# State-space heads whose two column groups work in pairs, and an FF down projection with the gated activations stationary

## The chip, the cores and the metric

One core of one Trainium2 chip runs the whole program in one launch. The metric is the device time of an execution in microseconds (us), lower is better. Five engines work side by side: PE (matmuls; its weight loads are shown apart as PEld), DVE (vector operations), ACT (activation functions and copies), POOL (hardly used here) and SP (which issues the DMAs).

## The reference, cut to what matters

Two transformer-like blocks run one after the other on 256 tokens of width 1024: first two layers with a mixture of experts, then one layer with three mixers (mLSTM, attention, state space) and a feed-forward net (FF). Only the last two parts are touched.

```python
def ssd_scan(x, dt, a_coef, bm, cm, state, emit):     # 8 heads of width 64, in 2 groups, two directions
    ...
        xdt = xk * dtk[..., None]
        seg = jnp.exp(jnp.where(causal, s[:, :, None] - s[:, None], -jnp.inf))
        y = (jnp.einsum('btsh,bshp->bthp', jnp.einsum('bthn,bshn->btsh', ch, bh) * seg, xdt)
             + jnp.exp(s)[..., None] * jnp.einsum('bthn,bhpn->bthp', ch, h))

def conv_ffn(h, w_up, conv_w, w_down):                # D_FF = 2816
    a, g = jnp.split(dwconv(h @ w_up, conv_w), 2, axis=-1)
    return (jax.nn.silu(g) * a) @ w_down

        h2 = modulate_2(rmsnorm_2(x, norm2_g[l]), mod[3][:, None], mod[4][:, None])
        x = x + mod[5][:, None] * conv_ffn(h2, w_up[l], ffn_conv_w[l], w_down[l])
```

## The kernel before, in words

Activations are held features by tokens (`x` is 128 partitions x 8 x 256). Every engine has its own program, written out by hand in one order; semaphores tie them together. Weights come through a ring of six 1 MB slots that SP refills when a slot is released. Eight PSUM banks serve PE's results: banks 0 to 3 are handed round to ACT (`to_act`), banks 4 to 7 to DVE (`to_dve`); PE may fill a bank again when its reader has taken it (`fill`, `close`, `take`). A float32 matmul shows up as two rows of PE in the trace. An fp32r matmul is one row; there, weights and activations are split into a high and a low part (ACT makes the high one, L1994, DVE the low one, L2896), and `PASSES` multiplies three of the four combinations.

**State-space heads (L1345 to L1368).** For each of 8 heads `hd` and 2 directions `d` a 512 x 256 matrix of decays (4 tiles of 128 x 256) is made: PE spreads a row over the partitions (`s_rows`, L1241), DVE subtracts and caps (`s_least`, L2846), ACT takes the exponential (`s_exps`, L1974), DVE multiplies by the masked products of the head's group (`s_qm`, L2044; made by `mask`, L2630 to L2640). PE then multiplies each tile by the head's values (L1366): 64 output columns, 4 tiles, 2 directions, so 8 float32 matmuls a head, into partitions 0 to 63 for an even head and 64 to 127 for an odd one. DVE takes the result out (`s_out`, L2858). Between two heads PE computes one "spare" slot, a 256-column slice of the merge gates (`linear`, L596: 16 float32 matmuls 256 wide), whose two results ACT takes out with a tanh (L1516). `s_xd` is the values times the time step, 8 DVE operations ahead of head 0. At head 0 and head 4 the products of the next group are made (L1234).

**FF (L1403 to L1454).** After the norm (`norm_sum`, L687; ACT's L1531 and L1535; DVE's L2119; then the split of `h`, ACT L2012 and DVE L2940) PE runs 11 pairs of 128-wide hidden tiles: `up` (L1421) for two weight slots, 96 matmuls 256 wide, and then `down` (L1432) of the pair before, 48 matmuls 256 wide: the weights are stationary and the tokens move, and the results add up over all pairs in banks 4 to 7. Four matmuls of zeros (L1408, 8 rows) open these banks. DVE does the convolution and the gate (L2048, L2053) and writes `f_parts` (L2960, L2044), whose completion is the semaphore `ff_hidden`. After the last `down` DVE adds gate times result to `x` (L2053, 8 operations), PE turns `x` into token order (L1454, 16 transposes), ACT copies that to `o_tok` (L1516) and SP stores it (L1498, 4 DMAs).

## Time and profile before

| | before |
|---|---|
| median of 3 runs | 1795.87 us (1794.08 to 1800.66) |
| the profiled execution: its time | 1794.45 us |
| its span (first to last instruction) | 1792.7 us |
| mean granted TensorE clock | 0.988 of full |
| state-space head blocks (from the first value matmul) | 1434.0 to 1519.7 us of the span |
| FF pairs | 1595.57 to 1786.05 us |
| after the last FF matmul | 1786.05 to 1792.7 us |

All times in the rows below are us from the start of the span; a row of the timeline gives start, duration, engine, line, operation, tiles, shape and count, and in brackets the idle time ahead of it and what ended it. Matmuls are pipelined: the duration of a run of them includes the tail of the last, so their pace is better read from the start of one run to the start of the next.

### The profile page before, as it was taken

The numbers are of one execution on the slowest core, as the hardware profiler recorded it, in microseconds if no ns is written. First come the engines' busy times: TensorE is split into PE (matmuls) and PEld (weight loads), VectorE is DVE, ScalarE is ACT, GpSimd is POOL, SyncE is SP. The second block draws the span as 40 slices with busy tenths as digits, with TensorE's granted clock in tenths as the row PEclk, the third lists the DMA queues.
The fourth block names the chain that finished last, engine by engine and source line by source line (L and its number), as shares of the span: only waits on it lengthen the run. The fifth ranks groups of instructions, "written<-read, shape, count | busy, mean of one in ns | idle before, by whom it ended". The sixth has DMA issues, their size and how long they took to land.

```text
span 1792.7 us, 24286 instructions
## 1 busy us (share of the span) xinstructions
PE 1726.9 (96%) x9797; PEld 1379.6 (77%) x9797; DVE 1158.8 (65%) x1670; ACT 764.7 (43%) x997; POOL 0.2 (0%) x4
## 2 busy tenths in 40 slices
PE   6999899999998999999999989999999999999999
PEld 4798677777886867777778876996745877899998
DVE  3665644448996376644469977528865763679887
ACT  3534533336674344433356756324322442254443
POOL 0000000000000000000000000000000000000000
PEclk9999899999999999999999999999999999999999
DMA  9958667778894696777778971234641332455540
GB/s 353 289 187 297 243 257 280 278 278 312 335 347 166 227 323 230 272 292 278 278 298 323 345 253 51 91 118 141 235 141 50 115 94 94 148 182 188 188 165 25
DMA packets 179032, 393.02 MB, mean 219 GB/s; under 512 B 11365, under 2 KB 102232, under 8 KB 162536
## 3 DMA queue, kind: packets, MB, share of 16 engines
q1 hardware_dynamic: 177246, 390.10, 60.9%
q8 instruction: 78, 1.28, 0.3%
q10 hardware_dynamic: 1674, 1.36, 0.2%
q14 instruction: 34, 0.28, 0.0%
HBM read 390.39 MB, written 1.05 MB: 218 GB/s over the span
## 4 chain that ended last, share of the span: by engine, by line
PE 86%; DVE 6%; ACT 3%; DMA 3%; issue 1%; ACTq 0%; SPq 0%; DVEq 0%
PE bank L969 19%; PE bank L997 10%; PE bank L596 9%; PE bank L1421 7%; PE bank L1208 5%; PE bank L1432 3%; PE bank L981 3%; PE bank L623 3%; PE bank L732 3%; PE bank L640 3%; PE bank L791 2%; PE bank L687 2%; PE bank L656 2%; DMA ring<-in_gla_w_in_dram 2%; PE bank L1012 2%; PE bank L1366 1%
## 5 line engine op out<-in xcount | busy, mean ns | idle before, releaser
L2352 DVE TENSOR_TENSOR parts<-ring,parts 128x2048 fp32r<-128x2048 f32 x144 | 328.7, 2290 | 140.2 <-ACT parts L1722 138.9
L969 PE MATMUL bank<-parts 128*128 128x512 f32 x1536 | 360.4, 393 | 8.4 <-DVE parts L2352 3.3
L1722 ACT ACTIVATE parts<-ring 128x2048 fp32r<-128x2048 f32 x144 | 275.3, 1917 | 204.5 <-PE bank L969 135.6
L969 PEld LDWEIGHTS bank<-parts 128*128 128x128 f32 x1536 | 286.3, 189 | 76.0 <-issue 17.8
L1516 ACT ACTIVATE work<-bank 128x256 f32<-128x256 f32 (+3 forms) x223 | 97.5, 446 | 406.3 <-PE bank L596 66.2
L997 PE MATMUL bank<-parts 128*128 128x512 f32 x768 | 182.9, 396 | 5.7 <-DVE parts L2377 3.7
L997 PEld LDWEIGHTS bank<-parts 128*128 128x128 f32 x768 | 145.5, 191 | 40.4 <-DVE parts L2377 4.1
L596 PE MATMUL bank<-hh,ring 128*128 128x256 f32 x640 | 143.4, 383 | 2.9 <-ACT hh L1563 2.7
L596 PEld LDWEIGHTS bank<-hh,ring 128*128 128x128 f32 x640 | 122.0, 192 | 23.9 <-issue 7.4
L1421 PE MATMUL bank<-parts 128*128 128x256 f32 x1056 | 128.6, 283 | 1.4 <-DVE parts L2940 1.4
L1421 PEld LDWEIGHTS bank<-parts 128*128 128x128 f32 x1056 | 127.6, 192 | 2.2 <-issue 2.2
L2896 DVE TENSOR_TENSOR parts<-ring,parts 128x2048 fp32r<-128x2048 f32 x37 | 84.8, 2292 | 16.7 <-ACT parts L1994 16.2
L1208 PE MATMUL bank<-hh,ring 128*128 128x256 f32 (+1 forms) x256 | 86.6, 491 | 2.2 <-ACT work L1516 2.2
L1994 ACT ACTIVATE parts<-ring 128x2048 fp32r<-128x2048 f32 x37 | 70.7, 1910 | 33.3 <-PE bank L1432 23.8
L2053 DVE SCALAR_TENSOR_TENSOR work<-work,cols 128x256 f32<-128x256 f32 (+1 forms) x144 | 76.2, 529 | 5.1
L2044 DVE TENSOR_TENSOR work<-work 128x256 f32<-128x256 f32 (+10 forms) x122 | 68.8, 564 | 16.0 <-ACT work L1974 6.7
L1208 PEld LDWEIGHTS bank<-hh,ring 128*128 128x128 f32 x256 | 47.4, 190 | 39.6 <-issue 32.9
L2053 DVE SCALAR_TENSOR_TENSOR work<-work 128x256 f32<-128x256 f32 (+4 forms) x96 | 62.6, 653 | 10.1 <-ACT work L1516 3.8
L1432 PE MATMUL bank<-parts 128*128 128x256 f32 x528 | 65.0, 283 | 0.0
L1432 PEld LDWEIGHTS bank<-parts 128*128 128x128 f32 x528 | 64.1, 192 | 0.0
L2126 DVE TENSOR_TENSOR ring_low<-ring,work_rounded 128x1024 fp32r<-128x1024 f32 x36 | 42.5, 1221 | 26.1 <-ACT work_rounded L1594 26.0
L981 PE MATMUL bank<-ring,work 128*64 128x256 f32 x512 | 58.8, 382 | 0.0
(324 smaller groups left out, 2488.8 us busy)
## 6 DMA issues: line engine op xcount, KB each, us to landing
ring<-in_moe_w_gate_dram SPq DMA_DIRECT2D x64, 1024.0 KB, 6.4
ring<-in_moe_w_up_dram SPq DMA_DIRECT2D x64, 1024.0 KB, 7.5
ring<-in_moe_w_down_dram SPq DMA_DIRECT2D x64, 1024.0 KB, 7.0
ring<-in_ada_w_dram SPq DMA_DIRECT2D x48, 1024.0 KB, 7.8
ring<-in_w_in_dram SPq DMA_DIRECT2D x32, 1024.0 KB, 6.0
ring<-in_w_mod_dram SPq DMA_DIRECT2D x24, 1024.0 KB, 7.4
ring<-in_w_up_dram SPq DMA_DIRECT2D x22, 1024.0 KB, 4.9
ring<-in_gla_w_in_dram SPq DMA_DIRECT2D x12, 1024.0 KB, 7.8
```

The lines of the kernel that those rows point to most:

```text
L596: ins = pe.matmul(ps[:, 0:n], w[:, k, m * P:(m + 1) * P], rhs(k), start=k == 0, stop=k == kt - 1)
L969: ins = pe.matmul(bank[:, :], xg[:, a_, k, tile * P:(tile + 1) * P], w[b_][:, j, :], start=k == 0 and n == 0, stop=k == KT - 1 and n == 2)
L981: ins = pe.matmul(bank[64 * h_:64 * h_ + 64, 0:256], x_few[:, k, :], w[:, j, 256 * h_:256 * h_ + 256], start=k == 0, stop=k == KT - 1)
L997: ins = pe.matmul(y_bank(rank, b, n)[:, :], he_t[:, b, a_, q * P:(q + 1) * P], w[b_][:, j, n * 512:(n + 1) * 512], start=i == 0 and q == 0 ...
L1208: ins = pe.matmul(ps[:, 0:n], w[:, k, m * P:(m + 1) * P], rhs(k), start=k == 0, stop=k == KT - 1)
L1421: ins = pe.matmul(ps[:, 0:T], w[a_][:, k, m * P:(m + 1) * P], h_parts[:, b_, k, :], start=k == 0 and i == 0, stop=k == KT - 1 and i == 2)
L1432: ins = pe.matmul(banks[4 + m // 2][:, (m % 2) * T:(m % 2 + 1) * T], w[a_][:, q, m * P:(m + 1) * P], f_parts[:, b_, i % 2, q, :], start=False,
L1516: act.activation(dst, view, func, **kw).then_inc(tiles.taken, 1)
L1722: act.activation(moe_w[:, n % 3, 0, :], ring[:, g % RING, :], ACT.Identity)\
L2053: v(dve.scalar_tensor_tensor(out=o, in0=i0, scalar=sc, in1=i1, op0=op0, op1=op1), done)
L2352: dve.tensor_tensor(moe_w[:, n % 3, 1, :], ring[:, (MOE_AT[layer] + AT[key]) % RING, :], moe_w[:, n % 3, 0, :].bitcast(F32), sub).then_inc ...
L2896: dve.tensor_tensor(w_parts[:, n % 3, 1, :], ring[:, (ff0 + n) % RING, :], w_parts[:, n % 3, 0, :].bitcast(F32), sub).then_inc(sem("low_re ...
```

## The change

1. Heads: the outer loop runs over 9 steps. Step `s` works on direction 1 of head `s-1` and direction 0 of head `s`. The two lie in different halves of the columns, and their matmuls alternate. The fourth tile of either is 128 wide and not 256: the other half of it is masked to zero. So a step has 8 matmuls, 4 in the first and the last. The products of both groups are made ahead of head 0, the second mask lies in the free part of `hh`, and rows and results have fixed banks with semaphores of their own (`s_row`, `s_values`, `s_out`).
2. FF: `down` makes the activations (`f_parts`) stationary and moves the weights 512 wide: 24 matmuls a pair and not 48. The result is in token order, 2 x 2 banks. The first matmul of a bank clears it, so the matmuls of zeros and the memset behind them go.
3. The turn of `x` into token order is done in the pairs 1 to 4 (`tokens_turned`, 4 transposes each, taken by ACT), and the gate is spread over partitions in pairs 5 and 6 (`gate_spread`, 4 float32 matmuls each). At the end DVE multiplies each bank by the gate and adds it to `o_tok` (two operations 512 wide a bank), and SP stores it.

```diff
-            def s_rows(hd):
-                if hd % 4 == 0:
-                    g = hd // 4
-                    products(lambda st: s_x[:, 4 + g, st * P:(st + 1) * P], s_x[:, 6 + g, T:TC])
-                spread(to_dve, (row_r, P, 64 + hd), (row_r, P, 96 + hd))
-                marks["s_row", hd] = to_dve.n
+            def s_products(g):
+                products(lambda st: s_x[:, 4 + g, st * P:(st + 1) * P], s_x[:, 6 + g, T:TC])
...
+            def s_row_bank(step):
+                return banks[4 + (s_first + step % 2) % 4]
+            def s_out_bank(hd):
+                return banks[4 + (s_first + 2 + hd // 2 % 2) % 4]
...
+            def s_rows(step):
+                if step < 2:
+                    pe.wait_ge(to_dve.taken, s_first + step + 1)
+                else:
+                    pe.wait_ge(sem("s_least"), 2 * step - 3)
+                for i, (hd, d) in enumerate(((step - 1, 1), (step, 0))):
+                    if 0 <= hd < S_H:
+                        ins = pe.matmul(s_row_bank(step)[:, i * T:(i + 1) * T],
+                                        ident[:, 64 + 32 * d + hd:65 + 32 * d + hd].to_broadcast([P, P]), row_r[:, :],
+                                        start=True, stop=True)
+                ins.then_inc(sem("s_row"), 1)
+            S_ORDER = ((0, 1, 2, 3), (0, 1, 3, 2))
+            def s_values(step):
+                if step == 0:
+                    pe.wait_ge(sem("s_xd"), 8)
+                    pe.wait_ge(to_dve.taken, s_first + 4)
+                elif 4 <= step < S_H:
+                    pe.wait_ge(sem("s_out"), step - 3)
+                pe.wait_ge(sem("s_w"), min(2 * step + 1, 2 * S_H))
+                for i in range(4):
+                    for hd, d in ((step - 1, 1), (step, 0)):
+                        if 0 <= hd < S_H:
+                            st = S_ORDER[d][i]
+                            at = slice(0, T) if i < 3 else (slice(P, T), slice(0, P))[d]
+                            rows = slice(64 * (hd % 2), 64 * (hd % 2) + 64)
+                            ins = pe.matmul(s_out_bank(hd)[rows, at], s_xd[:, d, st, hd * 64:(hd + 1) * 64],
+                                            s_e[hd % 2][d][:, st, at], start=d == 0 and i == 0, stop=d == 1 and i == 3,
+                                            skip_group_check=True)
+                ins.then_inc(sem("s_values"), 1)
+            s_products(0)
+            s_products(1)
             s_rows(0)
-            for hd in range(S_H):
-                if hd + 1 < S_H:
-                    s_rows(hd + 1)
-                for _ in range(2 if hd == 0 else 1):
+            for step in range(S_H + 1):
+                if step == 0:
                     spare.pop(0)()
-                rows = slice(64 * (hd % 2), 64 * (hd % 2) + 64)
-                ps = to_dve.fill(pe)
-                if hd == 0:
-                    pe.wait_ge(sem("s_xd"), 8)
-                for d in range(2):
-                    pe.wait_ge(sem("s_w"), 2 * hd + d + 1)
-                    for st in range(4):
-                        ins = pe.matmul(ps[rows, 0:T], s_xd[:, d, st, hd * 64:(hd + 1) * 64], s_e[hd % 2][d][:, st, :],
-                                        start=st == 0 and d == 0, stop=st == 3 and d == 1)
-                close(to_dve, ins)
+                if step < S_H:
+                    s_rows(step + 1)
+                    spare.pop(0)()
+                s_values(step)
...
+                    linear("branch", to_dve, lambda k: y[:, k, :], T, kt=4, tiles=4,
+                           after={2: 6, 3: 8} if half == 0 and y is y_m else {})
...
-            pe.wait_ge(sem("f_zeros"), 1)
-            for b in range(4):
-                pe.matmul(banks[4 + b][:, :], f_zero[:, 0:P], f_zero[:, :], start=True, stop=False,
-                          skip_group_check=True)
...
+            def down_part(w, i, q, t, n, order):
+                for a_, b_ in order:
+                    ins = pe.matmul(banks[4 + 2 * t + n][:, :], f_parts[:, b_, i % 2, q, t * P:(t + 1) * P],
+                                    w[a_][:, q, n * 512:(n + 1) * 512], start=i == 0 and q == 0 and (a_, b_) == (0, 0),
+                                    stop=i == FF_PAIRS - 1 and q == 1 and (a_, b_) == (1, 0), skip_group_check=True)
+                return ins
...
-                for q in range(2):
-                    for m in range(KT):
-                        for a_, b_ in PASSES:
-                            ins = pe.matmul(banks[4 + m // 2][:, (m % 2) * T:(m % 2 + 1) * T],
-                                            w[a_][:, q, m * P:(m + 1) * P], f_parts[:, b_, i % 2, q, :], start=False,
-                                            stop=i == FF_PAIRS - 1 and q == 1 and a_ == 1, skip_group_check=True)
-                        if i == FF_PAIRS - 1 and q == 1 and m % 2:
+                if i < FF_PAIRS - 1:
+                    for q in range(2):
+                        for t in range(TT):
+                            for n in range(2):
+                                ins = down_part(w, i, q, t, n, PASSES)
+                    ins.then_inc(sem("ff_down_used"), 1)
+                else:
+                    for t in range(TT):
+                        for n in range(2):
+                            for q in range(2):
+                                ins = down_part(w, i, q, t, n, PASSES)
                             ins.then_inc(sem("ff_done"), 1)
...
+            def gate_spread(half):
+                ps = to_act.fill(pe)
+                for k in range(4):
+                    at = 40 + 4 * half + k
+                    ins = pe.matmul(ps[:, k * P:(k + 1) * P], mods[:, 2, at:at + 1].to_broadcast([P, P]), ident,
+                                    start=True, stop=True)
+                close(to_act, ins)
             for i in range(FF_PAIRS):
                 up("ff_a", first=i == 0)
                 up("ff_g")
                 if i:
                     down(i - 1)
+                if 1 <= i < 5:
+                    tokens_turned((i - 1) // 2, (i - 1) % 2)
+                elif 5 <= i < 7:
+                    gate_spread(i - 5)
             down(FF_PAIRS - 1)
...
-            for half in range(2):
-                for t in range(TT):
+            for t in range(TT):
+                for half in range(2):
                     at = slice(half * 512, (half + 1) * 512)
-                    sp.wait_ge(sem("act_tile_taken"), marks["out", half, t])
+                    sp.wait_ge(sem("x_final"), 2 * t + half + 1)
                     sp.dma_start(out[0, t * P:(t + 1) * P, at], o_tok[:, t, at]).then_inc(sem("stored"), 16)
...
+            def s_exps(step):
+                for hd, d in ((step - 1, 1), (step, 0)):
+                    if 0 <= hd < S_H:
+                        act.wait_ge(sem("s_least"), 2 * hd + d + 1)
+                        r = 64 + 32 * d + hd
+                        for st in range(4):
+                            e = s_e[hd % 2][d][:, st, :]
+                            act.activation(e, e, ACT.Exp, bias=col_c[:, st, r:r + 1]).then_inc(sem("s_exp"), 1)
...
+                if 1 <= i < 5:
+                    take(o_tok[:, (i - 1) // 2, (i - 1) % 2 * 512:(i - 1) % 2 * 512 + 512], n=512)
+                elif 5 <= i < 7:
+                    take(gate_row[:, (i - 5) * 512:(i - 4) * 512], n=512)
...
+            def s_masks(g):
+                for half in range(2):
+                    mask(s_masked[g], half, take())
+            def s_least(step):
+                for i, (hd, d) in enumerate(((step - 1, 1), (step, 0))):
+                    if 0 <= hd < S_H:
+                        r = 32 * d + hd
+                        rows = marks["s_row_bank"](step)[:, i * T:(i + 1) * T]
+                        dve.wait_ge(sem("s_row"), step + 1)
+                        v(dve.tensor_tensor(s_e[hd % 2][d], rows.unsqueeze(1).to_broadcast([P, 4, T]),
+                                            col_n[:, :, r:r + 1].to_broadcast([P, 4, T]), ALU.min), sem("s_least"))
+            def s_weights(step):
+                for hd, d in ((step - 1, 1), (step, 0)):
+                    if 0 <= hd < S_H:
+                        dve.wait_ge(sem("s_exp"), 8 * hd + 4 * d + 4)
+                        tt(s_e[hd % 2][d], s_e[hd % 2][d], s_masked[hd // 4][:, d], mul, done=sem("s_w"))
...
+            for step in range(S_H + 1):
+                s_weights(step)
+                if step > 1:
+                    s_out(step - 2)
+                elif step == 1:
+                    dve.wait_ge(sem("s_values"), 1)
+                if step < S_H:
+                    s_least(step + 1)
...
-            v(dve.memset(f_zero, 0.0), sem("f_zeros"))
...
-            for k in range(KT):
-                if k % 2 == 0:
-                    dve.wait_ge(sem("ff_done"), k // 2 + 1)
-                stt(x[:, k, :], banks[4 + k // 2][:, (k % 2) * T:(k % 2 + 1) * T], mods[:, 2, 40 + k:41 + k],
-                    x[:, k, :], mul, add, done=sem("x_final") if k % 4 == 3 else s["dve_step"])
+            dve.wait_ge(sem("act_tile_taken"), marks["f_rows"])
+            gated = f_c.rearrange("p j t -> p (j t)")[:, 0:512]
+            for t in range(TT):
+                for half in range(2):
+                    at = slice(half * 512, half * 512 + 512)
+                    dve.wait_ge(sem("ff_done"), 2 * t + half + 1)
+                    tt(gated, banks[4 + 2 * t + half], gate_row[:, at], mul)
+                    tt(o_tok[:, t, at], o_tok[:, t, at], gated, add, done=sem("x_final"))
```

`s_exps` and `s_least` go over the same two (head, direction) pairs of a step as `s_weights`; `tokens_turned` holds four transposes of `x` and the hand-over to ACT. The old tail of transposes goes.

How PE's order moves at the first two head blocks. Before, from the products on (L1234 products, L1241 rows, L596 spare slots, L1366 values; the banks are numbered):

```order
L1234 MATMUL bank6<-work 128x256 [waits dve_tile_taken]
L1241 MATMUL bank7<-work,con 128x256 [waits dve_tile_taken]
L1241 MATMUL bank4<-work,con 128x256 [waits dve_tile_taken]
L596 MATMUL bank2<-hh,ring 128x256 [waits act_tile_taken,slot_landed5]
...
L1366 MATMUL bank5<-work 64x256 [waits s_w,s_xd,dve_tile_taken]
L1366 MATMUL bank5<-work 64x256 x3
L1366 MATMUL bank5<-work 64x256 [waits s_w]
L1366 MATMUL bank5<-work 64x256 x3
L1241 MATMUL bank6<-work,con 128x256 [waits dve_tile_taken]
L1241 MATMUL bank6<-work,con 128x256
L596 MATMUL bank2<-hh,ring 128x256 [waits act_tile_taken,slot_landed1]
```

And in the changed kernel (L1237 products, L1371 rows, L599 spare slots, L1392 values), the same place, and a later step in which the two heads have banks of their own:

```order
L1237 MATMUL bank7<-work 128x256 [waits dve_tile_taken]
L1237 MATMUL bank4<-work 128x256 [waits dve_tile_taken]
L1371 MATMUL bank5<-work,con 128x256 [waits dve_tile_taken]
...
L1392 MATMUL bank7<-work 64x256 [waits s_w,dve_tile_taken,s_xd]
L1392 MATMUL bank7<-work 64x256 x2
L1392 MATMUL bank7<-work 64x128
L1371 MATMUL bank5<-work,con 128x256 [waits s_least]
L1371 MATMUL bank5<-work,con 128x256
L599 MATMUL bank2<-hh,ring 128x256 [waits act_tile_taken,slot_landed1]
...
L1392 MATMUL bank7<-work 64x256 [waits s_w]
L1392 MATMUL bank4<-work 64x256
```

The second group's products stand ahead of the first rows, the first value block has 4 matmuls (the last 128 wide) instead of 8, and from then on two heads alternate. The spare slots keep their place ahead of the blocks.

DVE at the same place, changed kernel (L2906 is `s_least`, L2686 to L2696 the masks, L2100 products with the time step, then the weights):

```order
L2906 TENSOR_TENSOR work<-bank,lam_p 128x1024 [waits s_row,dve_tile_taken]
L2686 COPY hh<-bank 128x2x256 [waits dve_tile_ready,s_least]
L2687 COPY hh<-bank 128x2x256 [waits dve_step]
...
L2696 TENSOR_TENSOR hh<-bank,con 128x128 [waits dve_step]
L2100 TENSOR_TENSOR work<-work 128x512 [waits act_tile_taken,dve_tile_taken]
L2100 TENSOR_TENSOR work<-work 128x512 [waits s_xd] x7
L2100 TENSOR_TENSOR work<-work 128x1024 [waits s_exp,s_xd]
L2906 TENSOR_TENSOR work<-bank,lam_p 128x1024 [waits s_row,s_w]
L2906 TENSOR_TENSOR work<-bank,lam_p 128x1024 [waits s_row,s_least]
```

Before, two `s_least` (L2846) stood ahead of the eight products, two weights followed, and the masks of the second group came at head 4:

```order
L2846 TENSOR_TENSOR work<-bank,lam_p 128x1024 [waits dve_tile_ready,dve_tile_taken]
L2846 TENSOR_TENSOR work<-bank,lam_p 128x1024 [waits s_least]
L2044 TENSOR_TENSOR work<-work 128x512 [waits act_tile_taken,dve_tile_taken]
L2044 TENSOR_TENSOR work<-work 128x512 [waits s_xd] x7
L2044 TENSOR_TENSOR work<-work 128x1024 [waits s_exp,s_xd]
L2044 TENSOR_TENSOR work<-work 128x1024 [waits s_exp,s_w]
L2846 TENSOR_TENSOR work<-bank,lam_p 128x1024 [waits dve_tile_ready,s_w]
```

So the masks of the second group now stand ahead of `s_xd`, and one `s_least` and one weight less do.

## Rows read from the trace of the kernel before

**Rows 1.** The page: busy shares of the engines.
```profile
PE 1726.9 (96%) x9797; PEld 1379.6 (77%) x9797; DVE 1158.8 (65%) x1670; ACT 764.7 (43%) x997; POOL 0.2 (0%) x4
```
**Rows 2.** Windows, busy us (x instructions) of PE, PEld, DVE, ACT, POOL, clock, DMA.
```profile
1434.00:1519.70 85.70, 85.50 (x385) 64.85 (x384) 43.27 (x53) 31.24 (x76) 0.00 (x0) 1.00 0.29 94
1595.57:1786.05 190.48, 190.48 (x1584) 190.28 (x1584) 165.46 (x262) 83.41 (x99) 0.00 (x0) 1.00 0.41 139
```
**Rows 3.** Timeline of PE, the first head blocks.
```profile
1418.37 1.89 PE L1241 MATMUL bank<-work,con 128*128 128x256 f32 x8
1420.10 13.98 PE L596 MATMUL bank<-hh,ring 128*128 128x256 f32 x64
1434.01 3.67 PE L1366 MATMUL bank<-work 128*64 128x256 f32 x16
...
1438.94 7.14 PE L596 MATMUL bank<-hh,ring 128*128 128x256 f32 x32 [0.20 <-ACT work L1516]
1446.01 3.67 PE L1366 MATMUL bank<-work 128*64 128x256 f32 x16
1449.61 1.13 PE L1241 MATMUL bank<-work,con 128*128 128x256 f32 x4
```
**Rows 4.** Timeline of PE, expert stage: paired column groups, transposes, 512-wide fp32r.
```profile
249.87 1.09 PE L1022 MATMUL bank<-con,hh 128*128 128x128 f32 x8
250.89 3.67 PE L981 MATMUL bank<-ring,work 128*64 128x256 f32 x32
254.49 11.18 PE L997 MATMUL bank<-parts 128*128 128x512 f32 x48
265.51 0.38 PE L1030 MATMUL bank<-con,work 128*128 128x128 f32 x2
```
**Rows 5.** Timeline of DVE and ACT around the first head block.
```profile
1417.78 0.69 DVE L2630 COPY work<-bank 128x512 f32<-128x512 f32 x1 [0.31 <-PE bank L1234]
1421.70 2.48 DVE L2846 TENSOR_TENSOR work<-bank,lam_p 128x1024 f32<-128x1024 f32 x2
1424.21 8.29 DVE L2044 TENSOR_TENSOR work<-work 128x512 f32<-128x512 f32 x10
1433.80 3.30 ACT L1974 ACTIVATE work<-work 128x256 f32<-128x256 f32 x8 [7.54 <-DVE work L2846]
1437.12 1.28 ACT L1516 ACT_TABLE_LOAD   x1
1438.41 1.21 ACT L1516 ACTIVATE work<-bank 128x256 f32<-128x256 f32 x4
```
**Rows 6.** Timeline of PE and DVE, the last FF pairs.
```profile
1762.85 11.68 PE L1421 MATMUL bank<-parts 128*128 128x256 f32 x96
1774.37 11.68 PE L1432 MATMUL bank<-parts 128*128 128x256 f32 x96
1779.50 0.42 DVE L2044 TENSOR_TENSOR parts<-work,parts 128x256 fp32r<-128x256 f32 x1
```
**Rows 7.** Timeline of all engines after the last FF matmul.
```profile
1788.94 1.23 ACT L1516 ACTIVATE work<-bank 128x512 f32<-128x512 f32 x2 [0.85 <-PE bank L1454]
```
**Rows 8.** Timeline of PE, the FF norm.
```profile
1587.09 3.62 PE L687 MATMUL bank<-work,con 128*128 128x256 f32 x16
1590.54 3.60 PE L1408 MATMUL bank<-work 128*128 128x512 f32 x8
1595.57 0.71 PE L1421 MATMUL bank<-parts 128*128 128x256 f32 x4 [1.43 <-DVE parts L2940]
```
**Rows 9.** Windows around idle stretches of PE; the seventh number is the granted clock.
```profile
922.41:923.63 1.22, 0.00 (x0) 0.00 (x0) 1.22 (x1) 1.18 (x2) 0.00 (x0) 1.00 1.01 416
923.64:927.05 3.41, 3.00 (x7) 2.45 (x8) 3.41 (x4) 1.20 (x1) 0.00 (x0) 0.50 0.99 393
196.60:203.43 6.83, 6.35 (x29) 2.42 (x32) 6.03 (x21) 0.47 (x1) 0.00 (x0) 0.50 0.01 2
1322.53:1340.00 17.47, 15.27 (x40) 6.86 (x41) 10.54 (x25) 5.75 (x14) 0.00 (x0) 1.00 0.20 60
```

More of the change, by code:

```diff
@@ L586, in close, with linear @@
                 banks_.step()
-            def linear(what, to, rhs, n, kt=KT, tiles=2, first=False):
+            def linear(what, to, rhs, n, kt=KT, tiles=2, first=False, after={}):
                 w = weights(what, kt)
@@ L1445, in _ @@
                     down(i - 1)
+                if 1 <= i < 5:
+                    tokens_turned((i - 1) // 2, (i - 1) % 2)
+                elif 5 <= i < 7:
+                    gate_spread(i - 5)
             down(FF_PAIRS - 1)
-            for half in range(2):
-                pe.wait_ge(sem("x_final"), half + 1)
-                for t in range(TT):
-                    ps = to_act.fill(pe)
-                    for k in range(4):
-                        ins = pe.transpose(ps[:, k * P:(k + 1) * P], x[:, 4 * half + k, t * P:(t + 1) * P], ident)
-                    close(to_act, ins)
-                    marks["out", half, t] = to_act.n
             assert slot[0] == len(SLOTS)
@@ L2027, in _ @@
                 high(SPLIT_AT[i][2])
-            for half in range(2):
-                for t in range(TT):
-                    take(o_tok[:, t, half * 512:(half + 1) * 512], n=512, done=True)
+                if 1 <= i < 5:
+                    take(o_tok[:, (i - 1) // 2, (i - 1) % 2 * 512:(i - 1) % 2 * 512 + 512], n=512)
+                elif 5 <= i < 7:
+                    take(gate_row[:, (i - 5) * 512:(i - 4) * 512], n=512)
+            marks["f_rows"] = tiles.n
         @block.vector
@@ L2856, in s_out @@
                 rows = slice(64 * (hd % 2), 64 * (hd % 2) + 64)
-                ps = take()
-                took(dve.tensor_scalar(s_y[rows, j, :], ps[rows, 0:T], 0.125, None, mul))
+                dve.wait_ge(sem("s_values"), hd + 2)
+                ts(s_y[rows, j, :], marks["s_out_bank"](hd)[rows, 0:T], 0.125, None, mul, done=sem("s_out"))
                 if hd % 2:
@@ L2870, in _ @@
                     tt(s_xd[:, d, st, :].rearrange("p (h n) -> p h n", h=S_H), xt, dt, mul, done=sem("s_xd"))
-            for hd in range(S_H):
-                for d in range(2):
-                    dve.wait_ge(sem("s_exp"), 8 * hd + 4 * d + 4)
-                    tt(s_e[hd % 2][d], s_e[hd % 2][d], s_qm[:, d], mul, done=sem("s_w"))
-                if hd:
-                    s_out(hd - 1)
-                if hd + 1 < S_H:
-                    s_least(hd + 1)
+            for step in range(S_H + 1):
+                s_weights(step)
[3 more added lines that the diff above has]
+                    dve.wait_ge(sem("s_values"), 1)
+                if step < S_H:
+                    s_least(step + 1)
             s_out(S_H - 1)
```

56 lines of the change are left out of this document (20 added, 36 removed).

## The prediction

> **What bounds the kernel now.** I read the page first: PE is busy 96% of the span, the next engine 65% [rows 1]. Then the windows of the two stages that the change touches. In the head blocks PE is busy 85.50 of 85.70 us and DVE half of it; in the FF pairs PE is busy all 190.48 us, DVE 165.46 [rows 2]. Both stages end when PE has done its rows, so a PE row less is time less, as long as DVE (87% busy in the FF) and the hand-overs keep up. Then the timeline, for the pace of each kind of row and for the places where an engine is only just in time.
>
> **Heads: the value blocks.** A block is 16 rows (8 float32 matmuls) and takes 1449.61 - 1446.01 = 3.60 us [rows 3]; there are 8, so 28.8 us. A 256-wide row costs 0.216 us (8 rows in 1.73 us, L1241 [rows 3]), 16 of them 3.46, and 0.14 is the change-over. The expert stage shows what rows of 64 columns cost when two halves of the array alternate: 32 rows of the same size from 250.89 to 254.49, again 3.60 us [rows 4]. So a pair runs side by side, at half the price a row. A paired step has 16 rows, of which 4 are half as wide: 14/2 x 0.216 + 0.14 = 1.65 us. The first and the last step have 8 rows alone, worth 7: also 1.65. Nine steps make 14.9 us: **13.9 us less**. This leans on L981, whose pairs share one stationary operand; the new pairs share none. The bounds are 1.4 us a step (nothing for the change-over) and 3.2 us (no overlap at all, below). The products and the spare slots are as many as before and stand on the same path, so moving the second products costs nothing in sum; spreading rows costs the same 16 matmuls.
>
> **Heads: a new wait at the start.** The second group's masks, 3.92 us of DVE (1417.78 to 1421.70 is the first group's [rows 5]), now stand ahead of `s_xd`. DVE's sum from 1421.70: one `s_least` 1.24 (two take 2.48), masks 3.92, `s_xd` 5.77 (L2044 x10 takes 8.29, less two weights of 1.26), first weight 1.26: it is ready at 1433.9. PE gets there later than before by the products (1.73) less one row matmul (0.43): at 1435.3. No wait there. But DVE then makes the next two `s_least`, ready at 1435.15 and 1436.4; ACT's eight exponentials (0.41 each [rows 5]) end at about 1438.5. ACT must do them, and reload its table (1.28), before it takes the spare slot's results, so the load that stood at 1437.12 moves to 1438.5. Before, PE could go on 0.53 us after the first take (1438.41, then 1438.94 [rows 3, 5]), with 0.20 us idle. Now that is 1440.35, while PE wants the bank at 1435.3 + 1.65 + 0.86 = 1437.8. **2.3 us more idle.** Queued behind it are all of PE's later steps. Bounds: 0 (if ACT gets in a take between the exponentials, which its order forbids) and 3.5.
>
> After that nothing waits. A step of PE is 0.9 + 6.9 + 1.65 = 9.5 us. DVE does two `s_least`, two weights and 0.4 to 1.8 us of output, 6.8 us; from the end of one value block to the weights of the block after the next takes output 1.8, `s_least` 2.5, exponentials 2 more, weights 1.3, some 8 us of the 18 that PE needs. The last block waits for the same chain with one direction, 6 us of 9. The two new waits of the first merge linear are behind 3.5 us of PE work and ask for 1 us of DVE. **Heads: -11.6 us.**
>
> **FF: `down`.** 96 rows 256 wide take 1774.37 - 1762.85 = 11.52 us, 0.120 each [rows 6]; 48 are 5.76 us. 512 wide, stationary and moving operand from the same kind of tile, 48 rows take 265.51 - 254.49 = 11.02 us, 0.230 each [rows 4]; 24 are 5.51. Half the rows at nearly twice the price: 0.25 us a pair, 2.25 us for the first nine. The tenth gives only 0.1: the last `down` starts at 1780.13 now and needs `ff_hidden`, done at 1779.92 [rows 6], so PE meets DVE there. Bounds: twice 0.120 a row, which saves nothing, and 0.216, the price of a float32 row 256 wide [rows 3], which saves 5.7 us in all. The Trainium skill (TensorE: Matmul & The Clock Gate, Back-to-back issue gap) gives about 216 ns for a 512-wide matmul by itself; by that page, an estimate, the pairs would save those 5.7 us. The row of this kernel says 0.230, and I go by the row.
>
> **FF: what is added to PE.** 8 transposes of 128 x 128 take 1.02 us (249.87 to 250.89 [rows 4]). The 16 that leave the tail come back inside the loop, 2.0 us, and 8 float32 matmuls 128 wide, 16 rows, for the gate, another 2.0 by the same row. PE has no idle time there, so **4.1 us** are paid in full. ACT (83 of 190 us busy [rows 2]) takes 6 more tiles of 0.62 us (two in 1.23 [rows 7]); they come after a weight split and ahead of the first take of the next pair, with about 0.3 us to spare, and PE has four banks in hand. DVE has no new work in the loop.
>
> **FF: the norm.** The four zero matmuls fill 1590.54 to 1594.14 [rows 8] while PE waits for the split of `h` anyway, until 1595.57. Taking them away saves nothing. It leaves PE idle from 1590.71 for 4.9 us instead of 1.43. What that does is shown elsewhere: after 1.6 us without a matmul (1.22 ahead of 923.64, 3.41 - 3.00 behind it) the granted clock was 0.50 until 927.05, and once it stayed at 0.50 for 6.83 us; after 17.47 - 15.27 = 2.20 us without one at 1322.53 it stayed at 1.00 [rows 9]. So a shorter gap does it often, this one nearly surely. The half clock falls on rows that bound the stage: half of a stretch of 3.41 us is 1.7, less what falls into the gap, more if it lasts for two. **+1.7 us**, bounds 0 and 3.4. The Trainium skill warns of it (same page, HAM oscillation): a long pause of PE throttles what follows. By this rule alone the zeros were worth keeping; the trace agrees.
>
> **FF: the end.** From the start of the last `down` to the end were 1792.70 - 1780.13 = 12.57 us. Now the first bank is ready after 6 rows and the pipeline's tail, 1.6 us; DVE then has 8 operations 512 wide at 0.72 (the `s_xd` ones, 5.77 for 8; from PSUM a copy takes 0.69 [rows 5]), slightly more than PE's 1.38 a bank, so it ends at 7.4; and from the last operation to the end of the last DMA there were 1792.70 - 1790.17 = 2.53 us [rows 7]. Sum 9.9: **-2.7 us**.
>
> **Sum.** FF: -2.35 + 4.1 + 1.7 - 2.7 = +0.8. Heads -11.6. Together -10.8 us against the profiled execution's 1794.45 (span 1792.7 and 1.75 around it): 1783.6. The median of the three runs is 1.4 us above that execution, which would give 1785.1. I say 1784.
>
> **Rivals.**
> - *The pairs don't overlap* (each needs its own weights, and two of 64 columns must be loaded in the time of one row). Then a step of 16 rows costs 14 x 0.216 + 0.14 = 3.2, nine cost 25.5, the saving is 3.3: -3.3 + 2.3 + 0.8, so 1794. For it: no row of the trace has two different stationary tiles of this kind. Against it: each row of L981 loads its own as well. Chance 0.08.
> - *Slower: every change of column group drains the array.* Then a row costs its whole length, 3.67 - 15 x 0.216 = 0.43 [rows 3], and not 0.216: 7 x 14 x 0.43 + 2 x 7 x 0.216 = 45 us where 28.8 were, +16 + 3.1: 1814. It decides from 2.9 us a step on. Against it: L981 changes at every matmul and keeps its 3.60 us. The Trainium skill says that a change of tiling mode drains the engine and that tiles of one mode do not (TensorEngine Tiling, Key Properties); the 0.14 us of a block agrees with the first. Chance 0.03.
> - *The wait at the start comes back in each step*, because ACT does eight exponentials ahead of each take: 7 x 2 us, so 1796 to 1798. Against it: the table load happens once, and the chain has 8 of 18 us. Chance 0.06.
> - *The clock does not fall, or not on the path, and ACT's delay is smaller*: -13 to -16, 1778 to 1781. For it: the gap at 1322.53. Chance 0.15.
> - *A second clock drop*, from the new idle 2.5 us at 1438, or DVE falling behind in the FF (87% busy): 1787 to 1791. Chance 0.13.
> - The forecast, 1781 to 1787: 0.55.
>
> A measurement of this kernel can tell about 0.5%, 9.0 us, from no change: faster means under 1786.9. The forecast is only 2 us beyond it; most of its weight and that of the lower case are there: 0.64. Within 0.5%: the rest of it, most of the second clock case, the pairs that don't overlap, and the returning wait: 0.31. Slower 0.05. The range 1778 to 1791 leaves out the two rivals without a gain and the returning wait.
>
> **What will show it.** Value blocks of about 1.65 us from start to start, with rows of two halves beginning at nearly the same time; idle of some 2.5 us ahead of the second step's spare slot, ended by ACT, and none after; 24 rows of `down` in 5.5 us; a window of 0.50 clock at the start of `up`; the last DVE operation some 7.4 us after the last `down` starts. The prediction is wrong if a value block takes over 2 us, if PE idles in later steps, or if PE waits for `low_ready` in the pairs.

## The result and the profile after

The changed kernel takes 1786.47 us (median of 8 runs, 1783.41 to 1790.62) against 1796.8 us of the kernel before (8 runs, 1794.08 to 1800.66). The ratio is 0.9939, 95% interval 0.9927 to 0.9952, so 11.0 us less (0.0061 x 1796.8) where 10.8 were forecast; the two medians lie 10.3 us apart. One execution among the experiments, of ff_alone, took 2508 us where its others took 1796 to 1800; no comparison here uses it. The profiled execution has a span of 1783.3 us, before 1792.7.

The page's head and busy row, beside [rows 1]: PE has 256 rows less and is still 96% busy.

```profile
span 1783.3 us, 23776 instructions
PE 1712.4 (96%) x9541; PEld 1364.2 (77%) x9541; DVE 1160.8 (65%) x1669; ACT 765.7 (43%) x999; POOL 0.2 (0%) x4
```

The difference of two spans misleads here, since the part ahead of the changed stages, which no kernel here changes, moves by up to 7.1 us between executions, and the whole change is worth 11.0: the first transpose ahead of the state-space products (L1343, now L1346) begins at 1414.16 us before and at 1416.22 after, and in the nine kernels below anywhere up to 1421.30. So I cut each trace at three starts of PE: that transpose, the first merge matmul behind the heads, and the first matmul of the FF pairs. Lengths in us:

| kernel | heads | merge, w_out and norm | FF pairs to the end |
|---|---|---|---|
| before | 105.70 | 75.71 | 197.1 |
| after | 93.78 | 75.52 | 197.8 |
| heads_alone | 93.80 | 75.55 | 197.1 |
| ff_alone | 105.71 | 75.74 | 196.6 |
| serial | 100.19 | 75.73 | 197.7 |
| twos | 94.14 | 75.71 | 197.4 |
| full_tile | 95.50 | 75.72 | 196.6 |
| warm | 93.79 | 75.72 | 195.3 |
| take_first | 91.30 | 75.72 | 197.2 |
| both | 91.30 | 75.72 | 195.3 |
| in_gap | 91.30 | 75.72 | 191.8 |

The heads repeat within 0.02 us from kernel to kernel where their code is the same. Heads -11.92 (forecast -11.6), FF +0.65 (forecast +0.8), and -0.2 between them, where nothing was forecast. The last column also holds what the clock did: kernels with the same FF code (after, serial, twos, full_tile, take_first) differ there by up to 1.2 us.

The timeline of PE in the heads after the change, which answers to [rows 3] (columns as there):

```profile
1418.70 3.62 PE L1237 MATMUL bank<-work 128*128 128x256 f32 x16
...
1437.36 1.73 PE L1392 MATMUL bank<-work 128*64 128x256 f32 x8
1439.02 1.13 PE L1371 MATMUL bank<-work,con 128*128 128x256 f32 x4
1442.39 7.14 PE L599 MATMUL bank<-hh,ring 128*128 128x256 f32 x32 [2.25 <-ACT work L1571]
1449.47 1.74 PE L1392 MATMUL bank<-work 128*64 128x256 f32 x16
1451.13 1.13 PE L1371 MATMUL bank<-work,con 128*128 128x256 f32 x4
1452.10 7.07 PE L599 MATMUL bank<-hh,ring 128*128 128x256 f32 x32
1459.10 1.74 PE L1392 MATMUL bank<-work 128*64 128x256 f32 x16
1460.76 1.13 PE L1371 MATMUL bank<-work,con 128*128 128x256 f32 x4
```

A paired block of 16 rows takes 1451.13 - 1449.47 = 1.66 us from start to start, where 16 rows took 3.60; the single block of 8 rows takes 1.66 too (1437.36 to 1439.02). Both are the forecast 1.65. Ahead of the second step's spare slot stand 2.25 us of idle, ended by ACT: from the rows to the spare slot it is 1442.39 - 1439.02 = 3.37 us, in the later steps 1452.10 - 1451.13 = 0.97, and none of them has idle time. What ACT did then, to be read beside [rows 5]:

```profile
1437.26 3.30 ACT L2027 ACTIVATE work<-work 128x256 f32<-128x256 f32 x8 [10.54 <-DVE work L2906]
1440.57 1.28 ACT L1571 ACT_TABLE_LOAD   x1
1441.87 1.21 ACT L1571 ACTIVATE work<-bank 128x256 f32<-128x256 f32 x4
```

Eight exponentials, then the table load, then the first take at 1441.87; PE goes on 0.52 us later. Counted from the first transpose, the table load stands 24.35 us in (before: 22.96), as DVE has the second masks in between.

The FF, PE's timeline for one pair with transposes, one with the gate, and the last, to be read beside [rows 6]:

```profile
1663.49 5.63 PE L1463 MATMUL bank<-parts 128*128 128x512 f32 x24
1668.96 0.60 PE L1490 MATMUL bank<-con,x 128*128 128x128 f32 x4
1669.32 11.75 PE L1455 MATMUL bank<-parts 128*128 128x256 f32 x96
1680.91 5.63 PE L1463 MATMUL bank<-parts 128*128 128x512 f32 x24
1686.37 1.05 PE L1498 MATMUL bank<-con,mods 128*128 128x128 f32 x8
1687.18 11.76 PE L1455 MATMUL bank<-parts 128*128 128x256 f32 x96
...
1756.08 11.68 PE L1455 MATMUL bank<-parts 128*128 128x256 f32 x96
1767.59 11.41 PE L1463 MATMUL bank<-parts 128*128 128x512 f32 x48
```

24 wide rows take 1668.96 - 1663.49 = 5.47 us, where 48 took 5.76. Four transposes cost 0.36 us, eight gate rows 0.81, and the `up` behind them is 0.08 longer (1680.91 - 1669.32 = 11.59, without them 1767.59 - 1756.08 = 11.51). The last two `down` stand in one row; DVE's last write of `ff_hidden` ends at 1773.16 and the last `down` begins at 1773.30. The end, DVE's timeline:

```profile
1772.73 0.43 DVE L2100 TENSOR_TENSOR parts<-work,parts 128x256 fp32r<-128x256 f32 x1
1775.06 0.69 DVE L2100 TENSOR_TENSOR work<-bank,work 128x512 f32<-128x512 f32 x1 [1.91 <-PE bank L1463]
...
1780.14 0.69 DVE L2100 TENSOR_TENSOR work<-work 128x512 f32<-128x512 f32 x1
```

From 1773.30 to the end of the span at 1783.3 are 10.0 us (forecast 9.9, before 12.57). And the clock, windows of the changed kernel (the seventh number):

```profile
1580.66:1585.52 4.86, 0.00 (x1) 0.03 (x1) 3.80 (x10) 4.11 (x11) 0.00 (x0) 0.91 0.31 128
1585.52:1591.47 5.95, 5.95 (x28) 5.95 (x29) 4.86 (x9) 2.27 (x3) 0.00 (x0) 0.50 0.01 1
```

After 4.86 us without a matmul the granted clock is 0.50, that is 1.2 GHz, for the first 5.95 us of the pairs, in which PE starts 28 rows; at 0.120 us each they are 3.4 us of work.

### The profile page after: what moved, and what is told of

It is laid out like the page before. It is cut to its first block, busy times and chain, and to the rows that moved or that the text cites. A ratio compares the mean times of both kernels' runs of the same rounds, so it can differ in the third digit from the quotient of the medians.

```text
span 1783.3 us, 23776 instructions
## 1 busy us (share of the span) xinstructions
PE 1712.4 (96%) x9541; PEld 1364.2 (77%) x9541; DVE 1160.8 (65%) x1669; ACT 765.7 (43%) x999; POOL 0.2 (0%) x4
## 4 chain that ended last, share of the span: by engine, by line
PE 87%; DVE 6%; DMA 3%; ACT 3%; issue 1%; ACTq 0%; SPq 0%; DVEq 0%
PE bank L972 19%; PE bank L1000 10%; PE bank L599 9%; PE bank L1455 7%; PE bank L1211 5%; PE bank L984 3%; PE bank L626 3%; PE bank L1463 3%; PE bank L735 3%; PE bank L643 3%; PE bank L690 2%; PE bank L794 2%; DMA ring<-in_gla_w_in_dram 2%; PE bank L659 2%; PE bank L1015 2%; DVE parts L2408 1%
## 5 line engine op out<-in xcount | busy, mean ns | idle before, releaser
L972 PE MATMUL bank<-parts 128*128 128x512 f32 x1536 | 361.8, 394 | 10.3 <-DVE parts L2495 7.1
L972 PEld LDWEIGHTS bank<-parts 128*128 128x128 f32 x1536 | 287.3, 189 | 78.4 <-issue 19.7
L1000 PE MATMUL bank<-parts 128*128 128x512 f32 x768 | 182.9, 396 | 5.7 <-DVE parts L2433 3.7
L1000 PEld LDWEIGHTS bank<-parts 128*128 128x128 f32 x768 | 145.5, 191 | 40.4 <-DVE parts L2433 4.1
L599 PE MATMUL bank<-hh,ring 128*128 128x256 f32 x640 | 141.8, 380 | 4.5 <-ACT hh L1618 2.3
L599 PEld LDWEIGHTS bank<-hh,ring 128*128 128x128 f32 x640 | 120.9, 190 | 24.8 <-issue 8.6
L1455 PE MATMUL bank<-parts 128*128 128x256 f32 x1056 | 131.4, 287 | 4.9 <-DVE parts L3004 4.9
L1455 PEld LDWEIGHTS bank<-parts 128*128 128x128 f32 x1056 | 130.1, 195 | 5.5 <-issue 5.2
L2100 DVE TENSOR_TENSOR work<-work 128x256 f32<-128x256 f32 (+10 forms) x118 | 61.8, 524 | 12.8 <-ACT work L2027 3.4
L1463 PE MATMUL bank<-parts 128*128 128x512 f32 x264 | 62.0, 390 | 0.1
L1463 PEld LDWEIGHTS bank<-parts 128*128 128x128 f32 x264 | 48.9, 188 | 10.2 <-issue 0.5
```

The source lines that it names most:

```text
L599: ins = pe.matmul(ps[:, 0:n], w[:, k, m * P:(m + 1) * P], rhs(k), start=k == 0, stop=k == kt - 1)
L972: ins = pe.matmul(bank[:, :], xg[:, a_, k, tile * P:(tile + 1) * P], w[b_][:, j, :], start=k == 0 and n == 0, stop=k == KT - 1 and n == 2)
L1000: ins = pe.matmul(y_bank(rank, b, n)[:, :], he_t[:, b, a_, q * P:(q + 1) * P], w[b_][:, j, n * 512:(n + 1) * 512], start=i == 0 and q == 0 ...
L1455: ins = pe.matmul(ps[:, 0:T], w[a_][:, k, m * P:(m + 1) * P], h_parts[:, b_, k, :], start=k == 0 and i == 0, stop=k == KT - 1 and i == 2)
L1463: ins = pe.matmul(banks[4 + 2 * t + n][:, :], f_parts[:, b_, i % 2, q, t * P:(t + 1) * P], w[a_][:, q, n * 512:(n + 1) * 512], start=i == ...
```

## The experiments

Theory: the gain is the paired blocks alone; the FF change adds up to nothing, because what its wide matmuls and its short end bring is paid back by work in the loop and by the clock. Rivals: the FF has a gain of its own that luck hides; or the gain of the heads isn't the alternation.

**heads_alone** and **ff_alone**: the kernel before with one part of the change each.

```diff
  heads_alone: s_rows, s_values, s_exps, s_least, s_weights and the fixed banks; FF as before
  ff_alone:    down_part, tokens_turned, gate_spread, the new end, no matmuls of zeros; heads as before
```

> The kernel before with part 1 of the change only (the steps of the heads). By the theory that the gain is the pairing of the heads' value blocks and the rest adds up to nothing: the stage from the transposes ahead of the first products to the first merge linear falls by 11.9 us (14 in the blocks, 2.1 given back to the new wait), the end does not move, and the time is 1784.5 to 1786 against 1796.8 (ratio 0.993 to 0.994). By the rival that the FF change carried part of it (the clock's luck hides a gain there): under 8 us, ratio 0.996 or more. The norm keeps its matmuls of zeros, so the granted clock should be 1.00 at the start of the FF pairs.

> The kernel before with parts 2 and 3 of the change only (the FF). By the theory: nothing in sum. About 2.5 us less for the wider matmuls, 4.1 more for the transposes and the gate inside the loop, 1.7 to 3.4 more for the half clock after the idle norm, 2.8 less at the end: +0.5 to +2, ratio 1.000 to 1.001. By the rival that the wide matmuls are worth more than the pace of 0.230 us says: a gain of 3 us or more, ratio under 0.998. The profile should show 4.9 us idle ahead of the first matmul of the pairs and then a window of 0.50 clock.

Measured: heads_alone 1785.93 us (5 runs) against 1797.78 (16 runs of the kernel before), ratio 0.9931 (0.9918 to 0.9945), stage 93.80. ff_alone 1797.38 us, ratio 0.9999 (0.9990 to 1.0008). The heads carry all of it, and the FF is worth nothing in sum, both by the theory; ff_alone lies 0.4 us under the kernel before, where +0.5 to +2 were expected. In ff_alone the first matmul of the pairs also comes after 4.86 us of idle (PE's timeline), the half clock follows for 3.41 us, and the stage is 0.5 us shorter than before:

```profile
1601.46 2.83 PE L1416 MATMUL bank<-parts 128*128 128x256 f32 x13 [4.86 <-DVE parts L2958]
```

heads_alone, with the zeros in place, idles 1.43 us there and keeps the full clock.

**serial**: the changed kernel, the two heads of a step one after the other.

```diff
-                for i in range(4):
-                    for hd, d in ((step - 1, 1), (step, 0)):
+                for hd, d in ((step - 1, 1), (step, 0)):
+                    for i in range(4):
                         if 0 <= hd < S_H:
```

> The changed kernel, but in each step all four matmuls of the one head stand ahead of all four of the other; same work, same waits, same operands, no alternation. By the theory that alternation between the halves of the columns is what halves the price: a block of 16 rows goes from 1.66 to 3.1 or 3.2 us, seven of them, so +10 us (1796 to 1797, ratio to the kernel before 0.999 to 1.001). By the rival that PE overlaps what lies in different column groups wherever it stands in its queue: the block stays under 2.3 us and the time within 3 us of the changed kernel's.

Measured: 1791.61 us (5 runs), ratio 0.9972 (0.9957 to 0.9988), stage 100.19, that is 6.4 us more than alternating. Neither number came. PE's timeline:

```profile
1451.72 2.65 PE L1392 MATMUL bank<-work 128*64 128x256 f32 x16
1454.30 1.13 PE L1371 MATMUL bank<-work,con 128*128 128x256 f32 x4
```

A block takes 2.58 us, between 1.66 and the 3.17 of no overlap (14 x 0.216 + 0.14). The single rows of the trace show why. They don't name their head, but each head has six rows 256 wide and then two 128 wide, and the first row of either is longer than the others (0.43 us to 0.38), which leaves one reading: the first head's rows begin at 1451.720, 1451.986, 1452.202, 1452.418 and 1452.634, and at 1452.640, 0.92 us in, a row of the second head begins, although three of the first head's eight stand ahead of it in the program and begin later (1452.850, 1453.065, 1453.175). It is the same 0.92 us in all seven paired blocks. So PE lets a row of the other column group pass three that wait, and it did not pass four.

**twos**: two matmuls of one head, then two of the other.

```diff
-                for i in range(4):
-                    for hd, d in ((step - 1, 1), (step, 0)):
+                for hd, d, i in [(*g, 2 * h + i) for h in range(2) for g in ((step - 1, 1), (step, 0)) for i in range(2)]:
+                    if True:
                         if 0 <= hd < S_H:
```

> The changed kernel with the alternation coarser: two matmuls of one head, then two of the other, in every paired step. In the serial run the second head's first row began 0.92 us after the first head's, while four of the first head's rows were still to begin: PE looks some four rows ahead. By the theory that it overlaps two column groups as far as it looks ahead: two matmuls are four rows, so the second head starts at once or one row late, a block of 1.66 to 1.9 us and a head stage of 93.8 to 95.5 us. By the rival that only neighbours in the queue overlap, and serial's overlap was the tail of one: a block of 2.1 us or more, a stage of 97 us or more.

(The expectation counts four rows ahead; the single rows above say three.) Measured in a single execution: 1785.86 us, stage 94.14, and a block of 1461.49 - 1459.78 = 1.71 us:

```profile
1459.78 1.79 PE L1392 MATMUL bank<-work 128*64 128x256 f32 x16
1461.49 1.13 PE L1371 MATMUL bank<-work,con 128*128 128x256 f32 x4
```

The second head begins 0.013 us after the first, with three of the first one's four rows still to begin. The reach of three fits both runs; whether it is counted in rows or in something else isn't shown. The rival, neighbours only, is out.

**full_tile**: the fourth tiles 256 wide again, the masked half computed.

```diff
-                            at = slice(0, T) if i < 3 else (slice(P, T), slice(0, P))[d]
+                            at = slice(0, T)
```

> The changed kernel with the fourth tile of each head and direction 256 wide again (the masked half is computed, and adds zeros). By the theory: a block goes from 1.66 to 1.88 us, nine of them, +2.0 us: 1788 to 1789, ratio 0.995. By the rival that in a paired block the 128-wide rows cost as much as the wide ones (the weight load then sets the pace): no difference, block 1.66.

Measured: 1787.26 us (4 runs), ratio 0.9939 (0.9924 to 0.9954), which is the changed kernel's ratio too, and the time is under the expected 1788 to 1789; the stage tells them apart: 95.50, 1.72 more than the changed kernel. A block takes 1453.55 - 1451.67 = 1.88 us:

```profile
1444.59 7.14 PE L599 MATMUL bank<-hh,ring 128*128 128x256 f32 x32 [2.04 <-ACT work L1571]
1451.67 1.95 PE L1392 MATMUL bank<-work 128*64 128x256 f32 x16
1453.55 1.13 PE L1371 MATMUL bank<-work,con 128*128 128x256 f32 x4
```

Nine blocks at 0.22 are 2.0; 0.2 of it is taken from the idle ahead of the second spare slot, 2.04 in place of 2.25, since PE comes there later. Of the 13.9 us that the blocks lost, 2.0 are the narrow tiles, counted with the pairs in place, and the rest is the pairing.

**warm**: float32 matmuls of `x` by the identity where the zeros stood, their results thrown away.

```diff
             pe.wait_ge(to_dve.taken, to_dve.n)
+            for b in range(4):
+                pe.matmul(banks[4 + b][:, :], ident, x[:, 0:2, :].rearrange("p a t -> p (a t)"), start=True, stop=True,
+                          skip_group_check=True)
```

> The changed kernel with four float32 matmuls 512 wide put back where the matmuls of zeros stood (their results are thrown away), and no other work. By the theory that the idle norm costs 1.7 to 3.0 us through the clock: the granted clock stays at 1.00 there, the first 24 rows of the pairs take 2.9 us and not up to 5.5, and the time falls by about 2.3 us to 1783.5 to 1785, ratio 0.992 to 0.993. By the rival that the half clock is swallowed by slack (DVE and ACT behind PE): the clock rises but the FF stage keeps its length.

Measured: 1784.99 us (4 runs), ratio 0.9931 (0.9914 to 0.9947); the interval overlaps that of the changed kernel, so the stage must tell: 195.3 against 197.8, 2.5 us less. The window of the first 5.95 us, to be laid beside the one of the changed kernel:

```profile
1584.27:1590.22 5.95, 5.95 (x48) 5.95 (x49) 5.88 (x11) 2.28 (x3) 0.00 (x0) 1.00 0.02 3
```

48 rows where 28 began at the half clock. The rival, that slack swallows it, is out.

**take_first**: ACT takes the first two spare slots before the second step's exponentials.

```diff
             for step in range(S_H + 1):
+                if step == 0:
+                    spare.pop(0)()
+                    spare.pop(0)()
                 if step < S_H:
                     s_exps(step + 1)
-                    for _ in range(2 if step == 0 else 1):
-                        spare.pop(0)()
+                if 0 < step < S_H:
+                    spare.pop(0)()
```

> The changed kernel with one order changed on ACT: the two spare slots ahead of the first value block are taken out before the second step's eight exponentials. By the theory that the new 2.25 us of idle come from ACT's exponentials and its table load standing ahead of those takes: the idle goes, the stage is 2.2 us shorter, 1784 to 1785. By the rival that the masks moved ahead on DVE are the cause and PE then waits for the weights of the second step (s_w) instead: idle of 1 us or more ahead of the second value block, gain under 1.2 us.

Measured: 1784.79 us (4 runs), ratio 0.9922 (0.9906 to 0.9939), stage 91.30, 2.5 us less. From the first products on PE has no idle time left in the heads. From the rows to the second step's spare slot it is 1444.73 - 1443.76 = 0.97 us, as in every other step:

```profile
1443.76 1.13 PE L1371 MATMUL bank<-work,con 128*128 128x256 f32 x4
1444.73 7.07 PE L599 MATMUL bank<-hh,ring 128*128 128x256 f32 x32
```

ACT's table load stands in a stretch where ACT had nothing to do:

```profile
1431.48 1.28 ACT L1571 ACT_TABLE_LOAD   x1
1432.77 0.38 ACT L1571 ACTIVATE work<-bank 128x256 f32<-128x256 f32 x1
...
1442.49 3.29 ACT L2027 ACTIVATE work<-work 128x256 f32<-128x256 f32 x8
```

Counted from the first transpose the exponentials begin 21.5 us in (changed kernel: 21.0), and nobody waits for them. DVE still makes its masks at the old place, so they were not the cause by themselves.

**both**: warm and take_first together.

> The changes of warm and take_first together. By the theory that the two costs are in different stages and add up: 4 to 5 us under the changed kernel, 1781 to 1782.5, ratio 0.991. By the rival that the run-to-run luck of the clock hides them: indistinguishable from the changed kernel.

Measured: 1780.72 us (4 runs), ratio 0.9910 (0.9894 to 0.9927), stages 91.30 and 195.3: each stage has the length that its own edit gave it alone. The time is 0.3 us under the expected range; the rival, no difference, is out.

**in_gap**: take_first, and all transposes and gate matmuls moved from the pairs into the idle norm. The core of it, on PE:

```diff
             pe.wait_ge(to_dve.taken, to_dve.n)
+            for half in range(2):
+                for k in range(4):
+                    at = 40 + 4 * half + k
+                    ins = pe.matmul(banks[4 + half][:, k * P:(k + 1) * P], mods[:, 2, at:at + 1].to_broadcast([P, P]),
+                                    ident, start=True, stop=True)
+                ins.then_inc(sem("held"), 1)
+            for half in range(2):
+                for k in range(4):
+                    ins = pe.transpose(banks[6 + half][:, k * P:(k + 1) * P], x[:, 4 * half + k, 0:P], ident)
+                ins.then_inc(sem("held"), 1)
+            for half in range(2):
+                ps = to_act.fill(pe)
+                for k in range(4):
+                    ins = pe.transpose(ps[:, k * P:(k + 1) * P], x[:, 4 * half + k, P:T], ident)
+                close(to_act, ins)
```

ACT copies the last two out right after the split of `h` and the four of banks 4 to 7 during the first pair; the first `down` waits for these.

> The changed kernel with ACT's order of take_first, and with all six pieces of work that stood in the FF pairs (16 transposes, the gate's 8 float32 matmuls) moved into the idle norm: four of them into banks 4 to 7, which ACT copies out during the first pair, two through banks 0 to 3. By the theory: 4.1 us of PE work leave a loop that is bound by PE and fill an idle stretch of 4.9 us, the clock stays up (another 1.7 to 3.0), the wait in the heads goes (2.2): 8 to 9 us under the changed kernel, 1777 to 1778.5, ratio 0.988 to 0.990. By the rival that ACT's copies delay the first pair (its takes stand behind 3.7 us of copies) or that PE's loop then meets DVE: idle of PE in the first pairs, gain 6 us or less.

Measured: 1777.08 us (4 runs) against 1798.46 (7 runs), ratio 0.9887 (0.9870 to 0.9903); stages 91.30 and 191.8. Its FF stage is 3.5 us shorter than that of the kernel of the run before, warm and take_first together. PE in the norm:

```profile
1574.06 3.62 PE L690 MATMUL bank<-work,con 128*128 128x256 f32 x16
1577.51 1.95 PE L1448 MATMUL bank<-con,mods 128*128 128x128 f32 x16
1579.29 1.04 PE L1453 MATMUL bank<-con,x 128*128 128x128 f32 x8
1580.16 1.04 PE L1458 MATMUL bank<-con,x 128*128 128x128 f32 x8
1582.53 9.67 PE L1470 MATMUL bank<-parts 128*128 128x256 f32 x77 [1.33 <-DVE parts L3028]
```

The idle time is down to 1.33 us, no row of the half clock follows, and PE has no idle time in the pairs up to the last `down`, which meets DVE as in the changed kernel.

## Why the prediction was right

- **The value blocks**: 13.9 us forecast, 8 x 3.60 - 9 x 1.66 = 13.9 measured. L981 was the right row to lean on although its pairs share a stationary operand. It makes no difference whether the two heads write one bank (heads 0 and 1, 1449.47) or two (heads 1 and 2, 1460.76 - 1459.10 = 1.66). heads_alone carries the whole gain, and serial shows that with the same work and the same waits the order alone is worth 6.4 us. What I had not foreseen is that another 7 x (3.17 - 2.58) = 4.1 us of overlap come without alternating.
- **The wait at the start**: 2.3 us forecast; from the rows to the spare slot it was 1438.94 - 1437.61 = 1.33 before ([rows 3], and the block of 3.60 ahead of it) and is 3.37, so 2.0 measured. take_first ties it to the order of ACT's takes: 2.5 us came back, the 3.37 - 0.97 = 2.4 of the wait and 0.08 in the slot behind it. That is more than the 2.0, since the kernel before had 1.33 - 0.97 = 0.4 of it already. The masks only moved the moment at which that order bites.
- **The wide `down`**: 0.25 us a pair forecast, 5.76 - 5.47 = 0.29 measured for nine of them; the tenth, which meets DVE, gives 5.76 - (1773.30 - 1767.59) = 0.05 (forecast 0.1). The row of the expert stage was the better guide than the 216 ns of the Trainium skill (TensorE: Matmul & The Clock Gate, Back-to-back issue gap): 24 rows took 0.228 each. No run takes the wide `down` by itself; its worth is read from the timelines of both kernels.
- **Work added in the loop**: 4.1 us forecast, 4 x 0.36 + 2 x 0.81 + 6 x 0.08 = 3.5 measured, and 3.5 by in_gap against both. The term was sized too large: a row of it costs 0.11 us with all that hangs on it, not the 0.128 of the row that priced it.
- **The clock**: 1.7 us forecast, 2.5 measured (warm). The half clock came in every trace without filler matmuls in the norm, twice for 3.41 us and four times for 6.83, of which 5.95 fell on rows in the changed kernel (with the zeros, or anything in their place, in none of five). But at half clock a row takes 0.212 us and not 0.240: 28 rows in 5.95. A row of this kind doesn't double, so such a stretch costs 0.43 of its length and not half (1 - 0.120 / 0.212). That 3.41 us cost 1.3 is shown by full_tile and ff_alone, whose FF is 1.3 longer than warm's. The Trainium skill's warning of long pauses (TensorE: Matmul & The Clock Gate, HAM oscillation) fits all six.
- **The end**: 2.7 us forecast, 12.57 - 10.0 = 2.6 measured.
- **The rivals**: pairs that don't overlap and a drain at each change of group are excluded by the 1.66 us blocks. The returning wait is excluded by the timeline, with none after the second step. So is the second clock drop: the granted clock stayed at 1.00 through the 2.25 us of idle and the heads behind it (1439.02 to 1510.00), and PE met DVE in the FF at the last `down` alone. The gain of 11.0 us lies 2 us beyond the 9.0 that the prediction took as the least that can be told, as the sum said; with 8 runs of each kernel the interval ends at 0.9952 and excludes no change.
- **Two side sums of the prediction don't come out.** In the rival of the drained array a paired step would lose its gain from (28.8 - 3.1 - 2 x 1.65) / 7 = 3.2 us on, and not from 2.9, since two of the nine steps don't alternate. The 5.7 us of the 216 ns case count ten pairs in full, though the tenth meets DVE. Neither enters the forecast.

The FF's sum by what was measured is -9 x 0.29 - 0.05 + 3.5 + 2.5 - 2.6 = +0.7. Two of its terms, the added work and the clock, were off by more than half a microsecond in opposite directions, so that it came out at the forecast +0.8 by luck as well. And it did so only because the half clock lasted for 6.83 us in that execution: the forecast priced a stretch of 3.41, and with such a stretch the same FF code takes 196.6 (ff_alone, full_tile), 0.5 less than before and 1.3 under the forecast.

## What to carry to other kernels

Matmuls of 64 output columns whose results lie in different halves of the partitions run side by side when no more than three waiting rows stand between them in the queue, also with nothing in common but the array; alternate them and pay half. A matmul that only seems useless may hold the clock up across a wait: before taking it away, see how long PE idles then, and move real work into the place, which pays twice. And where a slow reader serves two queues, put the take that frees a bank ahead of the work that nobody needs yet.

## What the runs showed of the hardware that I had not expected

- PE does not start matmuls strictly in the order of the program. In serial, a row of the second column group began before three rows of the first that stand ahead of it. The Trainium skill says of matmuls that they start and end in program order (TensorE: Matmul & The Clock Gate, The mechanism); its cases are not this one, and here the measurement decides: the block of 2.58 us is not to be had in order.
- The price of the half clock depends on the row. 256 columns in fp32r went from 0.120 to 0.212 us (warm and the changed kernel, 5.95 us each), 1.8 times; from start to start, by the single rows of the trace of the kernel before, 512 columns in fp32r (L969) went from 0.227 to 0.427, 1.9 times, and a float32 row 256 wide (L596) from 0.216 to 0.427, twice.
- The part of the program that no kernel here changes moved by up to 7.1 us between profiled executions (1414.16 to 1421.30 at the first transpose). The half clock alone doesn't explain it: warm and take_first both spent 47.8 us at it ahead of that transpose, which begins 6.2 us apart in them, and PE is idle 4.3 us more in the later one; the cause stays open. Stages cut at fixed instructions repeated within 0.02 us in the heads.
